# Moving the probability scaling of the first attention from VectorE to GpSimd

## The chip, the cores and the metric

One core of a Trainium2 chip runs the whole program as one launch. The metric is the device time of that launch in microseconds. Between kernels, medians of several runs are compared. One further execution of the kernel was recorded by the profiler, and all rows and durations below come from it.

The engines are called by the names the profile uses: PE is TensorE, PEld its weight loads, DVE is VectorE, ACT is ScalarE, POOL is GpSimd, SP is SyncE.

## What is computed

The reference is a chain of two models over 256 tokens of width 1024. The first has an RG-LRU mixer, a convolutional feed-forward part, a sparse attention mixer (`nsa_mixer`) and another feed-forward part. The second has two layers with a convolution branch, neighbourhood attention and grouped attention, and a gated feed-forward part. The change touches `nsa_mixer` only. Cut to what matters:

```python
q, kv = heads of (x @ w_in)              # 16 query heads of width 64, 4 key/value heads
gates = sigmoid(...)                     # three gates for each head and token
# branch 0: compressed keys (done before the loop that the change touches)
# branch 1: chosen key blocks; with 256 tokens every block is chosen
s = q @ k_sel.T - slope * dist
p = masked_softmax(s, dist >= 0)
o_sel = p @ v_sel
# branch 2: a window of 512 keys; with 256 tokens it holds all earlier keys
s = q @ k_win.T - slope * dist
p = masked_softmax(s, m_w)
o_win = p @ v_win
o = gates[0] * o_cmp + gates[1] * o_sel + gates[2] * o_win
```

For branches 1 and 2 the kernel multiplies each row of exponentials by one number, the reciprocal of the row's sum times the gate of that branch, head and token, so that the two products with the values can be added up in one PSUM bank.

## The kernel before, in words

Each engine has its own instruction stream, written out in its own function, and the streams meet at semaphores. Weights stream from HBM through a ring of four slots, which SP fills. Most stages are three-pass products of split weights: ACT rounds a job of weights (`w_hi`), DVE subtracts (`w_lo`, L1353), and PE multiplies (all by the helper at L579). In the feed-forward stages POOL splits the hidden activations into two parts (a cast at L520, a subtraction at L522). While `ffn_out0` and `nsa_out` run it also sums squares of the residual (L530, L534), and it issues a few small loads.

The attention loop of `nsa_mixer` is called `softmax` in each engine's stream. It walks over 16 **pairs**. A pair is two heads for one tile of 128 queries. Even pairs have query tile 0 and see 128 keys, odd pairs have query tile 1 and see 256 keys, and each head has two branches, so a pair holds four blocks of 128x128 or of 128x256. Two pairs make a **round** in this text. In step v of their loops the engines do:

- **PE:** the scores of pair v (into two PSUM banks; the two bank pairs of `score_pairs` alternate); on even v from 4 on, the products with the values of pairs v-4 and v-3 (one output bank); then the transposes of pair v-2 (L781), which wait on `prob_ready` and write `turn_pair`, of which there is only one.
- **DVE:** for pair v, two instructions that add slope times distance to the scores in PSUM (L1524) and one that takes the row maxima (L1535, signals `score_max`); then for pair v-1 the reciprocal of the four sums (L1545), its product with the gates (L1550), and four multiplications of a block by its factor (L1555), which signal `prob_ready` for each head.
- **ACT** (all by the helper at L1020): the copy of the transposed pair v-2 from PSUM (signals `turned_ready`), then four exponentials of pair v into `s_p`, each with its row sum (signals `prob_exp`); on odd v from 5 on, the copy of a finished output bank.
- **POOL:** nothing. It waits for the last output copy (`o_free`, L546) and then issues two loads (L548) for later work.

`s_p` has four places, two for each pair. So the exponentials of pair v overwrite those of pair v-2. ACT is safe to do so since its own copy of the transposed pair v-2 comes first in its stream:

```python
go(used_pair(pT[...]), used_pair(turn_pair, kind, q), ACT.Copy).then_inc(turned_ready, 1)
if v < pairs:
    act.wait_ge(score_max, base // 2 + v + 1)
```

`s_sum` and `s_rec` hold the sums and factors of two pairs.

The functions that the change touches, with the profile's line numbers:

Of the kernel before, what the change touches and what calls it, by code (L numbers as in the profile page):

```python
# [27 lines left out]
ALU = mybir.AluOpType  # L28
# [260 lines left out]
def program(nc, wstream, params_in, consts_in, rpb_in, c_in, x_in, out):  # L289
    ctx = ExitStack()  # L290
    with ctx:
# [3 lines left out]
        def sem(name):  # L295
            return ctx.enter_context(nc.semaphore(name))
# [120 lines left out]
        operand_ready = sem("operand_ready")  # L417
        act_operand_ready = sem("act_operand_ready")
        score_full, score_max, prob_exp, prob_ready = (sem(n) for n in ("score_full", "score_max", "prob_exp", "prob_ready"))
        turned_full, turned_ready, o_full, o_free = (sem(n) for n in ("turned_full", "turned_ready", "o_full", "o_free"))  # L420
        dve_step, act_step, pool_step = sem("dve_step"), sem("act_step"), sem("pool_step")
        c_landed, c_ready, mod_summed = sem("c_landed"), sem("c_ready"), sem("mod_summed")
# [85 lines left out]
        @block.gpsimd  # L508
        def _(pool):
            for e in range(2):  # L510
                nc.gpsimd.memset(mod_parts[:, :, e, :], 0.0).then_inc(pool_written, 1)
            pstep = Count()

            def split_hidden(stage, units, products, hidden, N):

                for n, j, i in steps(pool, units, (pstep, 2)):
                    for e in range(2):
                        hi, lo = (v[:, bass.ds(n * 2 + e, 1), :].rearrange("p a b -> p (a b)")[:, 0:N] for v in hidden)
                        pool.wait_ge(acc_free[2 + e], n + (USED[stage][2 + e] + 1))
                        nc.gpsimd.tensor_copy(hi, products[:, e, 0:N]).then_inc(pool_step, 1)  # L520
                        pool.wait_ge(pool_step, pstep.next())
                        nc.gpsimd.tensor_tensor(lo, products[:, e, 0:N], hi.bitcast(F32), ALU.subtract).then_inc(pool_written, 1)  # L522


            def sum_squares(stage):

                for m in range(KD):
                    b, n = out_bank(stage, m)
                    pool.wait_ge(acc_free[b], n + (USED[stage][b] + 1))
                    square = nc.gpsimd.tensor_tensor((sq_one if m else sq_sum), x[:, m, 0:S], x[:, m, 0:S], ALU.mult)  # L530
                    if m:
                        square.then_inc(pool_step, 1)
                        pool.wait_ge(pool_step, pstep.next())
                        square = nc.gpsimd.tensor_tensor(sq_sum, sq_sum, sq_one, ALU.add)  # L534
                    if m < KD - 1:
                        square.then_inc(pool_step, 1)
                        pool.wait_ge(pool_step, pstep.next())
                    else:
                        square.then_inc(squares_summed, 1)

            pool.wait_ge(operand_ready, KL)
            for s in range(2):
                pool.dma_start(n_c[s], c_in[s]).then_inc(c_landed, 16)
            split_hidden("ffn_in0", KF1 // 2, f_prod, f_hidden, S)
            sum_squares("ffn_out0")
            pool.wait_ge(o_free, len(attention_jobs()) // 4)  # L546
            for s in range(2):
                pool.dma_start(n_c[s], c_in[s]).then_inc(c_landed, 16)  # L548
            sum_squares("nsa_out")
            split_hidden("ffn_in1", KF1 // 2, f_prod, f_hidden, S)  # L550

            for l in range(DEPTH):
                pool.wait_ge(rpb_place, l + 1)
                pool.dma_start(a_rpb.rearrange("p a b -> p (a b)"), rpb_in[l]).then_inc(rpb_landed, 16)
                pool.wait_ge(rpb_landed, 16 * (l + 1))
                pool.wait_ge(consts_landed, 16)

                nc.gpsimd.tensor_tensor(a_rpb, a_rpb, con("na_mask", 0, GRID).unsqueeze(1).broadcast_to([P, 48, GRID]),
                                        ALU.add).then_inc(rpb_ready, 1)
                if l == 0:  # L560

                    pool.wait_ge(o_free, (len(attention_jobs()) + len(attention_jobs(0))) // 4)
                    for s in range(2):
                        pool.dma_start(a_c[s], c_in[s]).then_inc(c_landed, 16)
                    pool.wait_ge(acc_free[3], USED["branch01"][3] + 2)
                    pool.dma_start(m_c[0], c_in[0]).then_inc(c_landed, 16)
                for p, units in (("a", HALF_A), ("b", HALF_B)):
                    split_hidden(f"mlp_in{l}{p}", units, m_prod, m_hidden, S2 if l == 0 else S)
# [735 lines left out]
        def _(dve):  # L1304
# [3 lines left out]
            def link(ins):  # L1308

                ins.then_inc(dve_step, 1)  # L1310
                dve.wait_ge(dve_step, step.next())
# [195 lines left out]
            def softmax(layer=None):  # L1507

                jobs = attention_jobs(layer)
                pairs = len(jobs) // 2  # L1510
                base = jobs_done.base
                for v in range(pairs + 1):
                    if v < pairs:
                        kind, t, _, q = jobs[2 * v]
                        if kind == "na" and jobs[2 * v - 1][0] != "na":
                            dve.wait_ge(rpb_ready, layer + 1)
                        dve.wait_ge(score_full, base // 2 + v + 1)
                        if kind == "nsa":
                            nk = (q + 1) * P
                            c = con("causal", q * S, nk).unsqueeze(1).broadcast_to([P, 2, nk])  # L1520
                            for p in range(2):
                                slope = float(np.float32(2.0 ** (-8.0 * (head_of(kind, t, p) + 1) / HEADS)))
                                sc = used(score_pairs[v % 2][:, p, :], kind, q)
                                ins = V.scalar_tensor_tensor(out=sc, in0=c, scalar=slope, in1=sc, op0=ALU.mult, op1=ALU.add)  # L1524
                            link(ins)
                        if kind == "na" and q < 2:
                            for p in range(2):
                                head = 2 * t + p
                                bias = a_rpb[:, head * 6 + 2 - 2 * q:head * 6 + 6 - 2 * q, :].rearrange("p a b -> p (a b)")
                                sc = score_pairs[v % 2][:, p, 0:S]  # L1530
                                ins = V.tensor_tensor(sc, sc, bias, ALU.add)
                            link(ins)
                        i = (v % 2) * 4
                        top = s_max[:, i:i + 4] if kind == "nsa" else s_max[:, i:i + 4:2]
                        ins = V.tensor_reduce(top, used_pair(score_pairs[v % 2], kind, q), AX, ALU.max, negate=True)  # L1535
                        if kind == "gqa":
                            link(ins)
                            ins = V.tensor_tensor(top, top, head_root[:, 8 * q + 2 * t:8 * q + 2 * t + 2], ALU.mult)
                        ins.then_inc(score_max, 1)
                    if v >= 1:  # L1540
                        kind, t, _, q = jobs[2 * v - 2]
                        i = ((v - 1) % 2) * 4
                        dve.wait_ge(prob_exp, base + 2 * v)
                        r_ = s_rec[:, i:i + 4] if kind == "nsa" else s_rec[:, i:i + 4:2]
                        link(V.reciprocal(r_, s_sum[:, i:i + 4] if kind == "nsa" else s_sum[:, i:i + 4:2]))  # L1545
                        if kind == "nsa":

                            g = n_gate[:, q, HEADS:3 * HEADS].rearrange("p (b h) -> p h b", b=2)[:, head_of(kind, t, 0):head_of(kind, t, 1) + 1:GROUP, :]
                            r2 = r_.rearrange("p (h b) -> p h b", b=2)
                            link(V.tensor_tensor(r2, r2, g, ALU.mult))  # L1550
                        for p in range(2):
                            o = used(s_p[:, (2 * v - 2 + p) % 4, :], kind, q)
                            for br in range(2 if kind == "nsa" else 1):
                                c = i + 2 * p + br
                                ins = V.tensor_scalar(o[:, br, :], o[:, br, :], s_rec[:, c:c + 1], None, ALU.mult)  # L1555
                            ins.then_inc(prob_ready, 1)
                jobs_done.base += len(jobs)

            ffn(0)
# [413 lines left out]
```

## Time and profile before

| | |
|---|---|
| median of 3 runs | 2247.96 us (2245.68 to 2248.45) |
| the profiled execution | 2248.55 us, of which 2246.7 us is the span of the trace |
| PE busy | 2103.2 us (94% of the span) |
| DVE busy | 1514.9 us (67%) |
| ACT busy | 875.6 us (39%) |
| POOL busy | 249.5 us (11%), 231 instructions |
| first attention | about 449.5 to 511 us of the span |

The span is the time from the first to the last recorded instruction. The busy shares are averages over the whole program and say little about a stage of some 60 us. For that, the trace is asked for the chain of waits and for the instructions in that stretch.

### The profile page before, as it was taken

The numbers are of one execution on the slowest core, as the hardware profiler recorded it, in microseconds if no ns is written. First come the engines' busy times: TensorE is split into PE (matmuls) and PEld (weight loads), VectorE is DVE, ScalarE is ACT, GpSimd is POOL, SyncE is SP. The second block draws the span as 40 slices with busy tenths as digits, with TensorE's granted clock in tenths as the row PEclk, the third lists the DMA queues.
The fourth block names the chain that finished last, engine by engine and source line by source line (L and its number), as shares of the span: only waits on it lengthen the run. The fifth ranks groups of instructions, "written<-read, shape, count | busy, mean of one in ns | idle before, by whom it ended". The sixth has DMA issues, their size and how long they took to land.

```text
span 2246.7 us, 33659 instructions
## 1 busy us (share of the span) xinstructions
PE 2103.2 (94%) x12858; PEld 1791.8 (80%) x12858; DVE 1514.9 (67%) x2859; ACT 875.6 (39%) x1376; POOL 249.5 (11%) x231
## 2 busy tenths in 40 slices
PE   7899999879999799889899989999997998999998
PEld 6789999748999588646567568888886865998998
DVE  7658898395888669776698863383276966355554
ACT  4634444273444432475211242212214336435443
POOL 0003321003330010000000002201211000001220
PEclk9999999889999899999999999999998999999999
DMA  6345465404556322103455422252243310344552
GB/s 234 121 175 190 179 248 209 149 1 165 188 179 260 134 95 76 57 1 132 152 213 207 170 111 94 93 193 107 94 169 123 131 57 20 151 176 162 186 187 78
DMA packets 46987, 318.09 MB, mean 142 GB/s; under 512 B 5008, under 2 KB 8080, under 8 KB 9488
## 3 DMA queue, kind: packets, MB, share of 16 engines
q1 hardware_dynamic: 45568, 309.58, 37.4%
q0 software_dynamic: 1296, 6.82, 0.8%
q8 instruction: 84, 1.38, 0.2%
q14 instruction: 39, 0.32, 0.0%
HBM read 315.33 MB, written 1.05 MB: 141 GB/s over the span
## 4 chain that ended last, share of the span: by engine, by line
PE 72%; DVE 17%; ACT 5%; issue 3%; DMA 2%; DVEq 0%; ACTq 0%; SPq 0%
PE ps L579 68%; DVE ps L1373 4%; DVE w_lo L1353 4%; ACT arena L1020 3%; DMA ring<-wstream 2%; PE ps L781 2%; PE ps L627 1%; DVE arena L1337 1%; DVE small L1535 1%; DVE rs L1319 1%; DVE arena L1555 1%; DVE h_lo L1347 1%; ACT w_hi L1020 1%; ACT L1020 1%; DVE ps L1524 1%
## 5 line engine op out<-in xcount | busy, mean ns | idle before, releaser
L579 PE MATMUL ps<-h_hi,w_hi 128*128 128x256 f32 (+1 forms) x2616 | 849.2, 325 | 48.7 <-DVE h_lo L1347 30.7
L579 PE MATMUL ps<-h_lo,w_hi 128*128 128x256 f32 (+1 forms) x2616 | 834.9, 319 | 0.0
L579 PE MATMUL ps<-h_hi,w_lo 128*128 128x256 f32 (+1 forms) x2616 | 833.8, 319 | 0.0
L1353 DVE TENSOR_TENSOR w_lo<-ring,w_hi 128x1024 fp32r<-128x1024 f32 x433 | 545.2, 1267 | 356.5 <-ACT w_hi L1020 355.7
L1020 ACT ACTIVATE w_hi<-ring 128x1024 fp32r<-128x1024 f32 x433 | 452.3, 1055 | 582.0 <-PE ps L579 476.6
L579 PEld LDWEIGHTS ps<-h_hi,w_hi 128*128 128x128 f32 x2616 | 503.0, 192 | 98.7 <-issue 42.9
L579 PEld LDWEIGHTS ps<-h_lo,w_hi 128*128 128x128 f32 x2616 | 504.6, 193 | 33.2 <-issue 1.2
L579 PEld LDWEIGHTS ps<-h_hi,w_lo 128*128 128x128 f32 x2616 | 504.5, 193 | 33.0
L1020 ACT ACTIVATE arena<-ps 128x512 f32<-128x512 f32 (+2 forms) x246 | 140.9, 575 | 461.1 <-PE ps L579 415.1
L1373 DVE SCALAR_TENSOR_TENSOR ps<-ring,arena 128x512 f32<-128x512 f32 x384 | 250.8, 725 | 0.0
L579 PE MATMUL ps<-arena,ring 128*128 128x256 f32 (+2 forms) x840 | 217.6, 420 | 20.6 <-DMA ring<-wstream 7.8
L579 PE MATMUL ps<-hid_hi,w_hi 128*128 128x256 f32 (+1 forms) x736 | 224.6, 305 | 0.9 <-DVE w_lo L1353 0.9
L579 PE MATMUL ps<-hid_lo,w_hi 128*128 128x256 f32 (+1 forms) x736 | 224.3, 305 | 0.0
L579 PE MATMUL ps<-hid_hi,w_lo 128*128 128x256 f32 (+1 forms) x736 | 224.3, 305 | 0.0
L579 PEld LDWEIGHTS ps<-arena,ring 128*128 128x128 f32 x840 | 150.9, 193 | 84.2 <-issue 54.5
L520 POOL CAST hid_hi<-arena 128x256 f32 (+3 forms) x92 | 82.5, 897 | 1024.8 <-DVE arena L1471 1024.8
L579 PE MATMUL ps<-arena 128*64 128x256 f32 (+4 forms) x800 | 129.5, 449 | 28.4 <-ACT arena L1020 24.7
L579 PEld LDWEIGHTS ps<-hid_hi,w_hi 128*128 128x128 f32 x736 | 138.4, 188 | 9.4 <-issue 1.2
L579 PEld LDWEIGHTS ps<-hid_lo,w_hi 128*128 128x128 f32 x736 | 138.1, 188 | 8.2
L579 PEld LDWEIGHTS ps<-hid_hi,w_lo 128*128 128x128 f32 x736 | 138.0, 188 | 8.1
L1687 DVE SCALAR_TENSOR_TENSOR arena<-arena,prm 128x512 f32<-128x512 f32 (+1 forms) x240 | 129.9, 613 | 0.4
L579 PEld LDWEIGHTS ps<-arena 128*64 128x64 f32 (+1 forms) x800 | 63.4, 174 | 70.4 <-issue 37.4
(153 smaller groups left out, 1673.3 us busy)
## 6 DMA issues: line engine op xcount, KB each, us to landing
ring<-wstream SPq DMA_DIRECT2D x290, 1024.0 KB, 4.8
arena<-c_in POOLq DMA_DIRECT2D x7, 512.0 KB, 4.5
arena<-rpb POOLq DMA_DIRECT2D x2, 1536.0 KB, 8.2
x<-x_in SPq DMA_DIRECT2D x2, 1024.0 KB, 12.1
out<-arena SPq DMA_DIRECT2D x8, 128.0 KB, 2.0
cst<-consts SPq DMA_DIRECT2D x1, 928.0 KB, 11.9
prm<-params SPq DMA_DIRECT2D x1, 580.0 KB, 10.6
ring<-wstream SPq DMA_DIRECT2D x1, 512.0 KB, 3.5
```

The lines of the kernel that those rows point to most:

```text
L520: nc.gpsimd.tensor_copy(hi, products[:, e, 0:N]).then_inc(pool_step, 1)
L579: ins = nc.tensor.matmul(*a, **k)
L627: ins = nc.tensor.matmul(psO[:, 0:N], ones[:], sq[:, k % 4, 0:N], start=k == 0, stop=k == KD - 1)
L781: ins = nc.tensor.transpose(turn_pair[:, p, b * P:(b + 1) * P], s_p[:, (2 * u + p) % 4, b * P:(b + 1) * P], ident)
L1020: return nc.scalar.activation(o, i, f, **k)
L1319: link(V.reciprocal(rs[:, 0:N], rs[:, 0:N]))
L1337: V.scalar_tensor_tensor(out=scaled[:, n % 8, :], in0=x[:, k, c], scalar=gain(k, s), in1=rs[:, c], op0=ALU.mult, op1=ALU.mult).then_inc(sc ...
L1347: ins = V.scalar_tensor_tensor(out=h_lo[:, k, c], in0=t, scalar=bias(k, s), in1=hi, op0=ALU.add, op1=ALU.subtract)
L1353: V.tensor_tensor(w_lo[:, job % SPLITS, :], raw_job(job), w_hi[:, job % SPLITS, :].bitcast(F32), ALU.subtract).then_inc(weights_ready, 1)
L1373: V.scalar_tensor_tensor(out=ps[4 + p][:], in0=w, scalar=1.0, in1=c[s][:, p * S2:(p + 1) * S2], op0=ALU.mult, op1=ALU.mult, accum_out=mod_ ...
L1524: ins = V.scalar_tensor_tensor(out=sc, in0=c, scalar=slope, in1=sc, op0=ALU.mult, op1=ALU.add)
L1687: return V.scalar_tensor_tensor(out=cy[:, c, 0:ns, :], in0=a_u3[:, c, 0:ns, bass.ds(j, S)], scalar=w, in1=cy[:, c, 0:ns, :], op0=ALU.mult, ...
```

## The change

POOL gets a loop over the 16 pairs. For each pair it waits for `factor_ready`, multiplies the four blocks of `s_p` by their factors in place, and signals `prob_ready` for each head. DVE no longer multiplies the blocks in this attention. It signals `factor_ready` at the gate product, without waiting for its own result, and from the third pair of factors on it waits until POOL has used the factors that it is about to overwrite. In the later attentions (kinds `gqa` and `na`) DVE multiplies as before.

```diff
+        factor_ready = sem("factor_ready")
...
             sum_squares("ffn_out0")
+            nsa_jobs = attention_jobs()
+            for v in range(len(nsa_jobs) // 2):
+                kind, _, _, q = nsa_jobs[2 * v]
+                pool.wait_ge(factor_ready, v + 1)
+                for p in range(2):
+                    o = used(s_p[:, (2 * v + p) % 4, :], kind, q)
+                    for br in range(2):
+                        c = (v % 2) * 4 + 2 * p + br
+                        ins = nc.gpsimd.tensor_scalar(o[:, br, :], o[:, br, :], s_rec[:, c:c + 1], None, ALU.mult)
+                    ins.then_inc(prob_ready, 1)
             pool.wait_ge(o_free, len(attention_jobs()) // 4)
...
                         dve.wait_ge(prob_exp, base + 2 * v)
+                        if kind == "nsa" and v >= 3:
+                            dve.wait_ge(prob_ready, 2 * v - 4)
...
-                            link(V.tensor_tensor(r2, r2, g, ALU.mult))
+                            V.tensor_tensor(r2, r2, g, ALU.mult).then_inc(factor_ready, 1)
+                        if kind == "nsa":
+                            continue
                         for p in range(2):
-                            o = used(s_p[:, (2 * v - 2 + p) % 4, :], kind, q)
-                            for br in range(2 if kind == "nsa" else 1):
-                                c = i + 2 * p + br
-                                ins = V.tensor_scalar(o[:, br, :], o[:, br, :], s_rec[:, c:c + 1], None, ALU.mult)
-                            ins.then_inc(prob_ready, 1)
+                            o, c = used(s_p[:, (2 * v - 2 + p) % 4, :], kind, q), i + 2 * p
+                            V.tensor_scalar(o[:, 0, :], o[:, 0, :], s_rec[:, c:c + 1], None, ALU.mult).then_inc(prob_ready, 1)
```

## Rows read from the trace of the kernel before

**Rows 1.** The page's chain that ended last, shares of the whole span.

```profile
PE 72%; DVE 17%; ACT 5%; issue 3%; DMA 2%; DVEq 0%; ACTq 0%; SPq 0%
```

**Rows 2.** Who waited for whom, 450 to 502 us: total us, times, longest.

```profile
PEld ps L781 <- DVE arena L1555: 11.7, 8, 1.9
```

**Rows 3.** The chain from 488 us on: start us, us, what ran.

```profile
488.50 0.88 DVE arena L1555 x4
489.37 0.68 DVE ps L1524 x2
...
490.08 0.69 DVE small L1535
...
490.89 0.17 DVE small L1550
...
491.09 1.14 DVE arena L1555 x4
...
495.00 0.88 DVE arena L1555 x4
...
501.22 1.94 ACT arena L1020 x8
...
503.60 1.15 DVE arena L1555 x4
...
504.80 1.11 PE ps L781 x8
...
507.09 3.52 PE ps L579 x20
...
510.63 0.39 ACT arena L1020
```

**Rows 4.** Timeline, ACT: start us, us, engine, line, operation, tiles, forms, [idle before <-releaser].

```profile
461.39 1.02 ACT L1020 ACTIVATE arena<-ps 128x1024 f32<-128x1024 f32 x1 [1.91 <-PE ps L781]
462.31 0.47 ACT L1020 ACTIVATE arena<-ps,small 128x256 f32<-128x256 f32 x1
```

**Rows 5.** Operations on the tile hid_hi, 540 to 780 us: ns min/median/max.

```profile
L520 POOL CAST hid_hi<-arena x24: 398/1274/1447, 554.7 to 681.3; 128x256 f32 x24
L522 POOL TENSOR_TENSOR hid_lo<-arena,hid_hi x24: 732/739/747, 556.1 to 681.9; 128x256 f32 x24
```

**Rows 6.** POOL's groups by form: xcount | busy us, mean ns | idle before.

```profile
L520 POOL CAST hid_hi<-arena 128x512 f32 x20 | 12.2, 612 | 369.1 <-DVE arena L1471 369.1
```

**Rows 7.** Timeline at 514 to 516 us, DVE and POOL.

```profile
514.83 0.42 DVE L1409 TENSOR_TENSOR x<-x,ps 128x256 f32<-128x256 f32 x1 [10.09 <-PE ps L579]
...
515.34 0.61 POOL L530 TENSOR_TENSOR arena<-x 128x256 f32<-128x256 f32 x1 [2.90 <-DVE x L1409]
```

**Rows 8.** Timeline in the second feed-forward part, DVE and POOL.

```profile
556.10 0.74 POOL L522 TENSOR_TENSOR hid_lo<-arena,hid_hi 128x256 f32 x1 [0.17 <-POOL hid_hi L520]
...
610.56 1.22 DVE L1353 TENSOR_TENSOR w_lo<-ring,w_hi 128x1024 fp32r<-128x1024 f32 x1
...
610.83 1.20 POOL L520 CAST hid_hi<-arena 128x256 f32 x1 [7.02 <-DVE arena L1471]
```

**Rows 9.** Timeline of PE through one round.

```profile
488.07 1.95 PE L579 MATMUL ps<-arena 128*64 128x256 f32 x20 [0.57 <-ACT arena L1020]
489.96 0.66 PE L781 MATMUL ps<-cst,arena 128*128 128x128 f32 x4
490.54 1.13 PE L579 MATMUL ps<-arena 64*128 64x512 f32 x4
492.28 1.09 PE L781 MATMUL ps<-cst,arena 128*128 128x128 f32 x8 [0.61 <-DVE arena L1555]
...
494.58 0.87 PE L579 MATMUL ps<-arena 128*64 128x256 f32 x6 [0.57 <-ACT arena L1020]
```

**Rows 10.** Windows of a round here and of a later attention: length, busy us of each engine, granted PE clock.

```profile
482.87:489.37 6.50, 5.32 (x42) 3.36 (x40) 6.29 (x19) 5.22 (x20) 0.00 (x0) 1.00 0.00 0
1014.00:1028.00 14.00, 9.90 (x68) 5.97 (x68) 7.43 (x20) 9.59 (x25) 0.00 (x0) 1.00 0.00 0
```

## The prediction

> **What bounds the kernel now.** I read the page's chain first, to see where DVE matters at all: PE carries 72% of it and DVE 17% [rows 1]. The chain cut to 488 us and later shows part of that 17%. Until 501.2 us it holds nothing but DVE: multiplications, bias, maxima, reciprocal, gates, and again [rows 3]. A round (one even and one odd pair) lasts from 488.50 to 495.00, so 6.50 us, of which the blocks' multiplications are 0.88 + 1.14 = 2.02 us. The waits say the same: in 52 us PE's transposes waited 11.7 us for DVE's multiplications [rows 2]. In one round of 6.50 us DVE is busy 6.29, PE 5.32, ACT 5.22 and POOL 0 [rows 10].
>
> So the tempting sum is 8 rounds by 2.02 us, 16 us less. It fails if something else stands close behind DVE. The chain after 501.22, where DVE has no scores left, shows what: exponentials, reciprocal, gates, multiplications, transposes, copy, one after the other [rows 3]. In the loop that string closes to a ring, because `s_p` has places for two pairs only. The exponentials of pair v come behind ACT's copy of pair v-2.
>
> **The ring, before.** For odd pairs, which are the larger: 2.38 from the first exponential at 501.22 to the multiplications at 503.60 (exponentials 1.94, the rest reciprocal and gates), 1.20 from there to the transposes at 504.80, transposes 1.11 [rows 3], and from the copy's start to the next exponential 0.92 [rows 4]. The sum is 5.61 us a round. It hides below DVE's 6.50 with 0.89 to spare.
>
> **The change, part by part.**
>
> *DVE* loses 2.02 us a round and its self-wait at the gate product, and stands at about 4.5. It is no bound any more.
>
> *The ring* loses the 1.20, and the self-wait of 0.03 between gate product and multiplications (490.89 and 0.17 to 491.09) [rows 3]. It gets: signal and wake-up of POOL 0.09 (515.34 less 514.83 and 0.42) [rows 7]; four POOL multiplications, 4t; and POOL's signal to PE. No row shows that signal. DVE's to PE takes 0.05 (504.80 less 503.60 and 1.15) [rows 3], and POOL's to itself 0.17 [rows 8]. I take 0.10 between them. The ring becomes 5.61 - 1.20 - 0.03 + 0.09 + 0.10 + 4t = **4.57 + 4t**. It equals the old round at t = 0.48 us.
>
> *The price t of a 128x256 multiplication on POOL* has no row. Nearest from below is the cast, also with one tensor in and one out: 0.40 where nothing disturbed it [rows 5]. From above, POOL's own multiply of two tensor inputs takes 0.61 [rows 7], and its subtraction 0.74 [rows 5]. The new instruction reads one tensor like the cast, but has a factor to fetch and an arithmetic step like the square. I can't place it nearer to either and take the middle, t = 0.505. For 128 columns: the cast takes 0.61 at 512 columns [rows 6] and 0.40 at 256, so 0.84 ns a column on 0.18, and 0.29 at 128. The square on the same 0.18 gives 0.40. The middle is 0.35.
>
> *The floor* without any POOL cost is a second loop, on PE. The value products start at 488.07 and take 1.89 to the even transposes at 489.96, then 0.58 to the odd scores, those 1.13, and from odd transposes to the next value products 2.30 (492.28 to 494.58) [rows 9]. That is 5.90 a round. The round can't become shorter than this whatever POOL costs.
>
> *The even ring* has exponentials, transposes and copy of half the width and is below the odd one. It costs nothing while the odd one binds.
>
> *Filling.* In the first steps PE paces the loop. There the first pair's multiplications lie open: 0.09 + 4 x 0.35 + 0.10 against 0.03 + 0.88 + 0.05, so +0.63.
>
> *Rounds.* From the exponentials of pair 3 at 462.31 [rows 4] to those of pair 15 at 501.22 [rows 3] there are six rounds in 38.91 us, 6.49 each. After: 4.57 + 4 x 0.505 = 6.59, so 6 x 0.10 = +0.6.
>
> *Emptying.* Behind the last exponentials the string lies open once: 0.09 + 0.10 + 2.02 = 2.21 against 1.23, so +0.98.
>
> *Waits and queues.* DVE's new wait on `prob_ready` stands ahead of a reciprocal, with the next pair's bias and maxima queued behind it. It asks for factors used two pairs ago, whose transposes have long run, so nothing. On POOL the two loads (L548) come behind the new loop, but they waited for the last output copy at 510.63 anyway. SP's queue is not touched and no transfer runs in this stretch (DMA share 0.00) [rows 10]. The stage after the attention starts on PE when the last output copy has ended, so a delay goes through to the end in full.
>
> **Sum:** 0.63 + 0.6 + 0.98 = **+2.2 us** on the execution's 2248.55. In t, with the 128-wide price moving along, it is nearly 28t - 12. The median of runs is 0.6 below that execution. I add to the median: 2250.2.
>
> **A page against the rows.** The four casts and squares above put POOL at 0.84 to 1.7 ns a column. The Trainium skill, GPSIMD Engine Reference, section "Elementwise — side-by-side cycle accounting", gives 1.8 cycles per element as the best case of a tight loop, at 1.2 GHz. By an estimate from that page the instruction would take 0.57 and 0.37 us with the 0.18 of the casts, and the sum would be +4.1, to 2252.1. The cast's rows disagree for one input (1.0 cycle by the same clock), and no run here shows a multiplication by a factor.
>
> **Rivals.**
>
> *POOL's ring becomes clearly longer than DVE's round.* It decides from t = 0.59. At the square's 0.61 the ring is 7.01: fill 4 x 0.40 + 0.19 - 0.96 = +0.8, rounds 6 x 0.52 = +3.1, end +1.4, together +5.3, to 2253.3. At the subtraction's 0.74 it is +9.3, to 2257.3, and a multiplication of 1 us would give some +17. For it: the arithmetic rows. Against: those read two tensors.
>
> *POOL and DVE get in each other's way.* Next to DVE's `w_lo` subtraction of two SBUF tensors a cast that takes 0.40 alone took 1.20 and ended with it [rows 8]. In the new loop DVE's gate product also has two SBUF inputs (factors and gates). If it met POOL's multiplications for the pair before, one would wait for an instruction of the other, up to t in every pair: about 6 x 0.5 + 0.5 = +3.5 on top, to 2253.7. Against it: gate products are 2.6 us apart (490.89, and 0.20 ahead of the multiplications at 488.50) [rows 3], and an even pair needs POOL for 1.4. The other DVE work reads PSUM and at most one SBUF tensor. The Trainium skill, SBUF — State Buffer, section "Who interferes with whom", has this as a lock for two-input instructions against a reading GpSimd. By this rule the trace agrees for the cast.
>
> *POOL costs little more than DVE did, t = 0.33 or less.* Then PE's loop binds: 6 x (5.90 - 6.49) = -3.5, with fill and end about +0.4, so -3.1, to 2244.9. For it: POOL idles here, with nothing to disturb it. Against: no row of POOL at 256 columns is below 0.40. At 0.40 itself the sum is -0.9. To be faster by more than 0.2% a part of the floor would have to be wrong.
>
> *PE's clock drops* if PE idles more. With a round of 6.6 PE is busy for 5.3, 80%. A later attention has PE busy 9.90 of 14.00 us at granted clock 1.00 [rows 10], so I give it little. The value products at the end, after a pause, took 3.52 us [rows 3] against 1.95 [rows 9]; such a PE would make the loop of 5.90 about 10 and cost some +21.
>
> **How the numbers follow.** About 0.2%, 4.5 us, is what a measurement of this kernel can tell from no change. Forecast (t between 0.40 and 0.58): 0.52. Cheaper, down to the floor: 0.05. POOL's price above 0.58: 0.33. The two-input conflict: 0.05. Clock: 0.02. Floor wrong and faster: 0.03. Same is 0.57, slower 0.40, faster 0.03. The range goes from 2245 (near the floor) to 2261 (t about 0.9), which leaves out some 0.12.
>
> **What would show it.** Right: DVE at about 4.5 busy in a round, with idle time ahead of the reciprocal; POOL's multiplications near 0.35 and 0.5; PE's transposes waiting for POOL; the chain going round exponentials, factors, POOL, transposes, copy; odd exponentials 6.6 us apart. Wrong: DVE still in the chain, PE waiting for copies alone (floor), POOL instructions stretched next to the gate products, or a granted clock below 1 in the steady part.

## The result, and the profile after

The changed kernel takes 2269.59 us (median of 4 runs, 2267.03 to 2271.24) against 2248.2 us for the kernel before in the same comparison. The ratio is 1.0094, with a 95% interval of 1.0077 to 1.0112. That is 21 us slower, where +2.2 was forecast and 2261 was the upper end of the range. In a second comparison, with 15 runs of the kernel before beside it, the ratio was 1.0081 (1.0067 to 1.0095): 18 us. The profiled execution of the first comparison has a span of 2265.2 us, 18.5 more than before. Both ratios lie far outside what the runs scatter by.

The price of the new instruction first. Groups of POOL by form, 440 to 530 us of the changed kernel (x count | busy us, mean ns | idle before it, and who ended the idle time):

```profile
L555 POOL TENSOR_SCALAR arena<-arena,small 128x256 f32<-128x256 f32 x32 | 29.0, 924 | 6.7 <-DVE small L1563 6.7
L555 POOL TENSOR_SCALAR arena<-arena,small 128x128 f32<-128x128 f32 x32 | 18.8, 604 | 109.3 <-DVE small L1563 109.3
```

A multiplication of 128x256 takes 0.92 us, of 128x128 0.60. Four in a row take 3.63 us, 0.91 each, since each starts a little before the last one has ended. Forecast were 0.505 and 0.35. The value does not lie between the cast's 0.40 and the subtraction's 0.74 [rows 5], but above both.

Now the chain of the changed kernel, one round and the start of the next (start us, us, what ran; three gaps of 0.02 are left out):

```profile
482.13 2.86 ACT arena L1031 x9
...
485.01 0.19 DVE small L1558
...
485.22 0.18 DVE small L1563
485.40 0.08 issue
485.48 3.63 POOL arena L555 x4
489.12 0.04 issue
489.16 1.11 PE ps L792 x8
...
490.29 2.86 ACT arena L1031 x9
```

This is the ring of the prediction, piece for piece: copy and exponentials, reciprocal, gate product, four POOL multiplications, transposes, copy again. It takes 490.29 - 482.13 = 8.16 us, where the chain of before went through DVE alone and took 6.50 [rows 3]. Without POOL's 3.63 it is 4.53; the forecast was 4.57. In the six rounds of the forecast DVE is busy for 4.3 to 4.8 us each, where about 4.5 was forecast.

Who waited for whom in the changed kernel, 450 to 525 us (total us, times, longest):

```profile
PEld ps L792 <- POOL arena L555: 24.6, 11, 3.5
...
DVE ps L1535 <- PE ps L590: 21.3, 13, 3.4
```

The transposes, which waited 11.7 us for DVE's multiplications before [rows 2], now wait 24.6 us for POOL's. DVE waited 1.9 us for scores before (450 to 512 us); now it is 21.3. It has been relieved and has nothing to do with the time it got.

Where the 18.5 us of the two spans lie: the attention, from the first scores on PE to the end of the last output copy, takes 61.5 us before (449.55 to 511.02) and 76.9 after (452.41 to 529.30). That is 15.4. The other 3.1 lie outside it: 2.9 ahead of the first scores, where the instructions are the same in both kernels, and 0.2 behind the last copy (1735.7 and 1735.9 us to the end of the span).

### The profile page after: what moved, and what is told of

Same layout as the page of the kernel before. It is cut to its first block, busy times and chain, and to the rows that moved or that the text cites. A ratio compares the mean times of both kernels' runs of the same rounds, so it can differ in the third digit from the quotient of the medians.

```text
span 2265.2 us, 33675 instructions
## 1 busy us (share of the span) xinstructions
PE 2111.5 (93%) x12858; PEld 1796.7 (79%) x12858; DVE 1499.5 (66%) x2795; ACT 875.6 (39%) x1376; POOL 297.0 (13%) x295
## 4 chain that ended last, share of the span: by engine, by line
PE 72%; DVE 16%; ACT 5%; issue 3%; DMA 2%; POOL 1%; DVEq 0%; ACTq 0%; SPq 0%
PE ps L590 68%; DVE ps L1384 4%; DVE w_lo L1364 4%; ACT arena L1031 4%; PE ps L792 2%; DMA ring<-wstream 2%; PE ps L638 1%; POOL arena L555 1%; DVE arena L1348 1%; DVE rs L1330 1%; DVE h_lo L1358 1%; ACT w_hi L1031 1%; ACT L1031 1%; DVE arena L1699 1%; DVE arena L1504 1%
## 5 line engine op out<-in xcount | busy, mean ns | idle before, releaser
L1031 ACT ACTIVATE w_hi<-ring 128x1024 fp32r<-128x1024 f32 x433 | 452.4, 1055 | 584.7 <-PE ps L590 478.3
L590 PE MATMUL ps<-arena 128*64 128x256 f32 (+4 forms) x800 | 135.9, 468 | 27.8 <-ACT arena L1031 23.8
```

The source lines that it names most:

```text
L590: ins = nc.tensor.matmul(*a, **k)
L1031: return nc.scalar.activation(o, i, f, **k)
```

## The experiments

The theory under test (A): the time of a round is that of a ring of some 4.5 us plus four POOL instructions, so the size of t explains the loss. Each profile gives the attention as above, and the round from the starts of the exponentials of odd pairs. Each kernel is compared with runs of the kernel before that were made beside it. Their median is 2250.83 us for the first four experiments, 2250.87 for the one with POOL on the even pairs and the three with three places, and 2250.63 for the others. The edits are shortened.

**POOL copies instead of multiplying.**

```diff
-ins = nc.gpsimd.tensor_scalar(o[:, br, :], o[:, br, :], s_rec[:, c:c + 1], None, ALU.mult)
+ins = nc.gpsimd.tensor_copy(o[:, br, :], o[:, br, :])
```

> The changed kernel, but GpSimd copies each block in place instead of multiplying it (it leaves out the scaling by reciprocal and gate). Theory A, a ring of 4.57 us plus four POOL instructions sets the round of two pairs: the cast form took 0.40 us for 128x256, so the ring is 6.2 us, the round 6.2 to 6.4 against 8.16 in the changed kernel, and the time returns to that of the kernel before, 2247 to 2250. Rival B, the work being on POOL at all is what costs (signals, a lock between the engines): the round stays near 8 and the time above 2262. Rival C, the lower clock of PE carries a third or more of the loss: the time stops near 2254.

Measured: 2250.96 us against 2250.83 before, ratio 1.000 (0.9991 to 1.001). Attention 60.0 us, round 6.19 on average over six. The signals and the work on POOL are all there and the loss is gone, so B has fallen; and the time does not stop near 2254, so C does not carry a third of the loss.

**A constant factor.**

```diff
-... s_rec[:, c:c + 1], None, ALU.mult)
+... 0.5, None, ALU.mult)
```

> The changed kernel with the constant 0.5 in place of the factor that is read from SBUF (it leaves out the scaling by reciprocal and gate). If fetching the factor is what makes the POOL instruction 0.90 us instead of the 0.40 of a cast, it falls to about 0.45 us, and the time to 2248 to 2251. If the multiply form itself is slow, it stays at 0.85 to 0.90 us for 256 columns, the round at 8.0 to 8.2 and the time at 2267 to 2271.

Measured: 2262.33 us, ratio 1.0051 (1.0034 to 1.0068). Attention 71.2, round 7.81. The time lies between the two answers that were written down.

**The tensor-tensor form.**

```diff
-ins = nc.gpsimd.tensor_scalar(o[:, br, :], o[:, br, :], s_rec[:, c:c + 1], None, ALU.mult)
+ins = nc.gpsimd.tensor_tensor(o[:, br, :], o[:, br, :], s_rec[:, c:c + 1].broadcast_to([P, (q + 1) * P]), ALU.mult)
```

> The changed kernel with the same product written as a tensor-tensor multiplication whose second input is the factor, repeated along the columns. Theory A with the price of the square seen before (0.61 us for 256 columns, about 0.40 for 128): ring 4.57 + 2.44 = 7.0 us, time about 2253.5, some 16 us better than the changed kernel. If POOL needs as long for it as for the scalar form (0.9 us), 2269.

Measured: 2256.55 us, ratio 1.0027 (1.0017 to 1.0038). Attention 65.7, round 6.85. It computes the same as the changed kernel in 12 us less (5.7 above the kernel before, where the changed kernel is 18.1 above it in the larger comparison).

The POOL groups of the three, in this order (x count | busy us, mean ns | idle before):

```profile
L555 POOL COPY arena<-arena 128x256 f32<-128x256 f32 x32 | 11.4, 401 | 8.8 <-DVE small L1563 8.8
L555 POOL COPY arena<-arena 128x128 f32<-128x128 f32 x32 | 8.0, 293 | 119.6 <-DVE small L1563 119.6
```

```profile
L555 POOL TENSOR_SCALAR arena<-arena 128x256 f32<-128x256 f32 x32 | 26.3, 848 | 7.2 <-DVE small L1563 7.1
L555 POOL TENSOR_SCALAR arena<-arena 128x128 f32<-128x128 f32 x32 | 16.1, 527 | 110.9 <-DVE small L1563 110.9
```

```profile
L555 POOL TENSOR_TENSOR arena<-arena,small 128x256 f32<-128x256 f32 x32 | 18.6, 615 | 7.5 <-DVE small L1563 7.5
L555 POOL TENSOR_TENSOR arena<-arena,small 128x128 f32<-128x128 f32 x32 | 11.8, 402 | 113.7 <-DVE small L1563 113.7
```

Each pair of rows gives a slope and a constant. Copy: 0.84 ns a column on 0.19 us. Two tensors: 1.66 on 0.19. Constant factor: 2.51 on 0.21. Factor from SBUF: 2.50 on 0.28. So fetching the factor costs 0.08 us an instruction, once; the rest of the high price is the scalar form's time per column, three times that of the copy.

And the four instructions in the chain of each, first with the constant factor, then with two tensors:

```profile
476.98 3.30 POOL arena L555 x4
...
484.79 3.30 POOL arena L555 x4
```

```profile
482.42 2.34 POOL arena L555 x4
...
489.27 2.34 POOL arena L555 x4
```

The rounds are 7.81 = 3.30 + 4.51, 6.85 = 2.34 (rounded) + 4.51, and 8.16 = 3.63 + 4.53. The formula holds over three prices with one constant. With the copy (four in 1.44 us) it would give 5.95. Three of the six rounds there took 5.93 or 5.94 and the other three 6.39 to 6.48, so another limit takes turns with it.

**POOL takes only the odd pairs, DVE the even ones** (with a semaphore of its own for each engine).

```diff
+                if not on_pool(v):        # on_pool(v) is v % 2 == 1
+                    continue
```

> GpSimd multiplies only the odd pairs (256 keys), VectorE the even ones. Theory A, the ring of the odd pairs binds and the even pairs on POOL cost only their exposed place at the start and a little queueing: 40% of POOL's work goes, the round stays at 8.16 us, the attention shortens from 76.9 to about 75 us, and the time is 2267 to 2268. Rival D, POOL's total work (5.96 us in a round) sets the pace: the round falls by about the 2.34 us taken away and the time to 2256 or less.

Measured: 2267.13 us, ratio 1.0073 (1.0057 to 1.009), within 2 us of the changed kernel's time, as expected. The timeline of ACT, the first exponential of two odd pairs in a row:

```profile
482.57 0.47 ACT L1044 ACTIVATE arena<-ps,small 128x256 f32<-128x256 f32 x1
...
490.74 0.47 ACT L1044 ACTIVATE arena<-ps,small 128x256 f32<-128x256 f32 x1
```

8.17 us. POOL does 3.6 us of work in a round instead of 5.96 and at most 2 us come back. D has fallen: the odd pairs' latency sets the pace, not POOL's load. (The attention took 78.2 us here rather than 75; four of its six rounds took 8.16 to 8.17 and the other two 8.66 and 8.44. Their granted clocks were 0.88 and 0.90, but a round of 8.17 had 0.89. What sets the two apart is where the stretch of lower clock fell: their odd transposes, which are part of the ring, took 1.59 and 1.37 us instead of 1.09, and that is all of the 0.50 and 0.28 that they are longer. From the first scores to the exponentials of pair 3 it took 15.1 us, against 14.1 and 14.9 in the two profiles of the changed kernel.)

**POOL takes only the even pairs, DVE the odd ones** (the same edit with `v % 2 == 0`).

> GpSimd multiplies only the even pairs (128 keys), VectorE the odd ones. Theory A: the odd ring is that of the kernel before (5.61 us), the even ring with four POOL instructions of 0.585 us is 5.5, VectorE is busy about 5.6 in a round, PE's loop takes 5.90. The round is 5.9 to 6.0 us against 6.49 before: -3.5 over six rounds, +1.6 for the first pair's exposed multiplications, together about -2, so 2245 to 2248. Rival B (any work on POOL costs) gives 2253 or more.

Measured: 2256.5 us, ratio 1.0025 (1.0014 to 1.0037), attention 65.4, round 7.09. I expected 5.9 and a gain. The time alone would fit B; the copy on POOL had ruled that out, and the chain of this kernel names what I had missed:

```profile
485.59 2.35 POOL arena L563 x4
487.94 0.04 issue
487.98 0.66 PE ps L805 x4
488.64 1.08 PE ps L598 x4
...
489.75 1.31 DVE ps L1548 x2
...
491.07 0.04 DVE small L1559
491.11 1.11 issue
492.21 0.18 DVE small L1571
...
492.42 0.18 DVE small L1576
...
492.67 2.35 POOL arena L563 x4
```

There is a second ring, made of instruction order. The even transposes wait for POOL. The next odd scores stand behind them in PE's stream. DVE's bias and maxima wait for those scores, and the next even pair's reciprocal stands behind them in DVE's stream. (The row of 1.11 us marked "issue" is the rest of the odd pair's maxima, which run from 491.07 for 1.22 us.) It takes 4.73 us plus POOL's four 128-wide multiplications, 7.08 in all.

**The same, with the even transposes behind the odd scores in PE's stream.**

```diff
-                    if 2 <= v < pairs + 2:
-                        u = v - 2
+                    for u in [v - 3, v - 2] if v % 2 else []:
```

> GpSimd on the even pairs only, as in the run where the round came out at 7.09 us instead of 5.9; but PE issues the even pair's transposes behind the next odd pair's scores instead of ahead of them. Theory F: in that run a second ring bound the round, which goes through PE's order: POOL's even multiplications 2.35, even transposes 0.66, odd scores 1.08, bias 1.30, maxima 1.15, reciprocal, gates, POOL again, 7.09 in all. With the transposes out of the scores' way it is cut: round 5.9 to 6.3, the attention 59 to 61.5 us instead of 65.4, the time within 2 us of the kernel before. If the loss there has another cause, the round stays near 7.

Measured: 2253.8 us, ratio 1.0014 (1.0005 to 1.0023), attention 63.2, round 6.69. The second ring is cut and POOL has left the chain, but only 0.4 us of a round came back and not 0.8 to 1.2, the attention missed the expected 59 to 61.5, and the time is 3.2 us above the kernel before and not within 2. The chain of this kernel now repeats ACT's exponentials, PE's scores and value products, transposes, exponentials.

```profile
485.05 2.42 ACT arena L1046 x9
...
487.61 3.01 PE ps L598 x24
490.62 0.60 PE ps L807 x4
```

So F holds for what bound that run, since POOL's multiplications are gone from the chain and the round is shorter; my number for what would bind next was too low.

**Three places of pairs instead of two, POOL on all pairs.** The third place lies in memory that is free by then; transposes, copies and value products come one pair later.

```diff
+        more_p = part(2048, 2, S2)
...
-                    if 2 <= v < pairs + 2:
-                        u = v - 2
+                    if lag <= v < pairs + lag:      # lag = 3
+                        u = v - lag
...
-s_p[:, (2 * u + p) % 4, ...]
+place(kind, 2 * u + p)[:, ...]                      # one of 6
```

> The changed kernel with three places of pairs for the probabilities instead of two, and transposes, copies and value products one pair later, so that the exponentials of a pair no longer wait for the pair two before but three before. POOL's instructions are as before. Theory A: the ring of 8.2 us now spans three pairs, that is about 5.5 us a round, and no longer binds; POOL itself does, with 5.96 us of work in a round, about 6.2 with its wake-ups. Six rounds of 2 us come back, so 12 of the 21 us: 2256 to 2259. If the ring is not what costs, the time stays at 2268 to 2272.

Measured: 2249.85 us against 2250.87, ratio 0.9997 (0.9988 to 1.0007). The attention is 63.2 us, the round 6.11. POOL's instructions cost as much as in the changed kernel (0.93 and 0.61 us), and by the medians all of the loss is gone, where 12 us of it were expected back. The round came out as expected. By the one profile the attention is 13.7 us shorter than in the changed kernel and still 1.7 to 3.2 longer than before; the rest of what the medians gained is not explained. The window 470 to 482 us of this kernel (length, busy us of PE, PEld, DVE, ACT, POOL, granted clock):

```profile
470.00:482.00 12.00, 10.39 (x82) 6.18 (x80) 8.95 (x20) 9.80 (x39) 11.90 (x17) 1.00 0.00 1
```

POOL is busy 11.90 of 12.00 us, so its throughput would allow no shorter round. But the chain of this kernel does not pass through POOL. It repeats PE's scores and value products (3.01 us), the even transposes, ACT's copy and exponentials, and PE again. Two limits have met here at 6.11 us.

**Three places, POOL on the even pairs only.**

> Both together: three places of pairs, GpSimd the even pairs only and VectorE the odd ones. Neither ring binds, POOL has 2.34 us in a round, VectorE 5.6, PE 5.3, ScalarE 5.2. Theory A: round 5.6 to 5.9 us against 6.49 before, 2243 to 2247, possibly the best of all. Rival: PE's loop over value products, transposes, scores and copy holds it at 5.9, then 2246.

Measured: 2251.51 us, ratio 1.0006 (0.9996 to 1.0015), attention 60.1, round 6.14. POOL is down to 4.70 of 12 us and the round is no shorter than with all pairs on POOL. Both numbers expected (5.6 to 5.9 or 5.9, and 2243 to 2247) were too low. The chain is the same loop of PE and ACT, and this run shows that it alone holds the round at 6.14:

```profile
485.45 3.01 PE ps L604 x24
488.46 0.60 PE ps L812 x4
...
489.08 0.56 ACT arena L1051
...
489.98 1.57 ACT arena L1051 x7
...
491.59 3.01 PE ps L604 x24
```

**Control: three places, DVE multiplies everything.**

> Control: the kernel before (VectorE multiplies everything) with three places of pairs. VectorE had 6.29 of 6.50 us busy in a round, so a longer ring gives nothing: 2247 to 2250, round 6.50. If the ring already cost something before, it is faster by 3 us or more.

Measured: 2253.3 us, ratio 1.0008 (0.9994 to 1.0022), round 6.50 as expected, attention 63.9. The deeper ring alone gives nothing. The time is 2.4 us above the kernel before and 3 above the range expected, and the attention 2.4 to 3.9 longer: the loop has an extra step at its ends, which the expectation left out. But the interval still includes no change.

**PE kept busy in the rounds.**

```diff
+                                if q == 1 and v >= 4:
+                                    mm(... the scores of this head, once more into the same bank)
                                 ins = mm(...
```

> The changed kernel with the scores of each odd pair from the fifth on computed twice into the same place, so that PE idles some 0.9 us less in a round, at a point of the round where nothing waits for it (odd transposes wait 2.26 us for POOL there). Theory A: PE's clock matters little inside the rounds; those that took 8.49 us become 8.16, so at best 1 us is gained, and the time stays within 1.5 us of the changed kernel. Rival C, the clock carries the part of the loss that the ring does not: the granted clock is 1.00 through the attention and 4 to 7 us come back.

Measured: 2267.28 us against 2268.73 for the changed kernel beside it; attention 76.6 us. The same window in the changed kernel, where it holds most of a slow round, and here (length, busy us of PE, PEld, DVE, ACT, POOL, granted clock):

```profile
494.00:506.00 12.00, 8.10 (x46) 4.45 (x47) 6.25 (x13) 7.11 (x28) 9.23 (x12) 0.86 0.00 1
```

```profile
494.00:506.00 12.00, 8.62 (x57) 4.84 (x56) 6.25 (x13) 7.11 (x28) 9.39 (x12) 1.00 0.01 2
```

The granted clock stays at 1.00 from 470 to 518 us and the rounds from 475 us on are all 8.16. The median is 1.4 us lower, with ranges that overlap (2264.7 to 2269.7, and 2266.3 to 2271.9 for the changed kernel), and the attention 0.3 and 0.7 us shorter than in the two profiles of the changed kernel. With the clock held up inside the rounds, 16.7 us of the loss are still there. C has fallen as a main cause.

**Both kernels profiled a second time.**

> The changed kernel once more, beside many runs of the kernel before on one chip. Its first profile puts 15.4 us of the loss inside the attention (76.9 against 61.5 us) and 3.1 us outside, at places that the change does not touch. Theory A: those 3.1 us are chance of one execution, so the medians differ by 15 to 18 us and the attention again takes 76 to 78 us. Rival E, something outside the attention is lost every time: 20 us or more, and again over 1788 us of span outside the attention.

> The kernel before once more, for a second profile. Theory A: attention 61.5 us, rounds of 6.50; outside the attention 1785 to 1790 us of span, as the kernels with and without work on POOL have shown. Rival E: 1785 again, below all kernels that use POOL.

Measured: the changed kernel 2268.73 us, 18.1 more than the 2250.63 beside it; attention 77.4 us. The kernel before: attention 60.0. The difference of the attentions is 17.4 us, that of the first profiles 15.4. Outside the attention the spans are 2185.2 and 2189.7 us (before), 2188.3 and 2192.2 (after), and 2184.6 to 2189.7 in the ten variants. (The two expectations say 1785 to 1790; they are 400 us too low by a slip in a subtraction.)

Where the difference outside lies can be told more closely. From the end of the last output copy to the end of the span it is 1735.7 and 1736.7 us before, 1735.9 and 1736.1 after. So nothing is lost behind the attention. What differs is the time up to the first scores: 449.6 and 453.1 us before, 452.4 and 456.1 after, 449.9 to 453.0 in the variants. No work was moved there, and the two values of one kernel lie 3.5 and 3.7 us apart, more than the kernels do. Of the signs of E, the loss of 20 us did not come (18.1), but the span outside was again above that of the kernel before (2192.2). I take the 3 us for chance; the 456.1 alone lies above all others, and it stays unexplained.

## Why the prediction was wrong

**The step that failed** is "the price t of a 128x256 multiplication on POOL". I put t at 0.505 between the cast and the square; the four take 3.63 us, 0.91 each. With that one number exchanged, and 0.59 for 128 columns, the same working gives: filling 0.09 + 2.35 + 0.10 - 0.96 = +1.6, rounds 6 x (4.57 + 3.63 - 6.49) = +10.3, emptying 0.19 + 3.63 - 1.23 = +2.6, together +14.4. Measured in the attention, first and second pair of profiles: filling +1.3 and +2.1, rounds +10.6 and +10.2, emptying +3.5 and +5.1, together +15.4 and +17.4. The bracketing was wrong in kind: I ordered the instructions by how many tensors they read, and the scalar form, with one input, is slower than both two-input forms.

**What held.** DVE bound the loop and is relieved of 2 us a round. The ring is the one of the prediction, in its parts and its constant (4.57 forecast, 4.53 measured). POOL's signals took 0.08 to start and 0.04 to PE, against 0.09 and 0.10. The two runs on either side of the break-even of 0.48 fit the working: the copy at 0.40 ends at no change, where -0.9 had been worked out, and the two-input form at 0.61 at +5.7 us, where it was +5.3. The fill does lie exposed: from the first scores to the exponentials of pair 3 it is 12.76 us before and 14.09 after, +1.33, or +2.1 in the second profiles.

**The Trainium skill against the rows.** The estimate from 1.8 cycles a column (the Trainium skill, GPSIMD Engine Reference, section "Elementwise — side-by-side cycle accounting") was 0.57 us for 256 columns. Measured were 0.92 us, with a slope of 2.5 ns a column, 3.0 cycles at the 1.2 GHz given there. For this instruction the measurement decides.

**Rivals.** The first one, POOL's ring becoming clearly longer than DVE's round, is what happened, with a price outside the rows that it was worked out from; the line "a multiplication of 1 us would give some +17" was the nearest. I ended the range at 2261, t of about 0.9. With the measured t the working gives 2262.4, just outside; the measured 2269.6 lies 7 us further on, of which what follows accounts for a part. The conflict between the engines did not come: no POOL multiplication took more than 0.93 us, and gate products keep their duration, but for one of 16 (DVE, operations on the factor tiles: ns min/median/max):

```profile
L1563 DVE TENSOR_TENSOR small<-small,arena x16: 165/166/316, 458.1 to 518.2; 128x4 f32<-128x4 f32 x16
```

Where POOL has the even pairs only, the odd pair's gate product ran beside one of its multiplications and took 0.28 us instead of 0.17, which is far from a wait of a whole multiplication. The argument for this rival misread its row in part: the cast [rows 8] ended at 612.03, 0.25 us behind the subtraction's end at 611.78, and not with it.

The clock came in part. Once the loop had filled, one transposing step of an odd pair took 1.43 us instead of 1.09, and the last one 1.98; the granted clock was 0.55 from 516 to 530 us. The rival's price of +21 has the size of the measured loss by coincidence only: in the run with the clock at 1.00 nearly all of the loss stayed. The slower last steps belong to the 1 to 3 us that the exchanged number leaves open. The chance of one execution belongs to it too, since the last value products of the kernel before took 3.50 us in its first profile and 1.95 in its second:

```profile
507.09 3.50 PE L579 MATMUL ps<-arena 128*64 128x256 f32 x20 [1.21 <-ACT arena L1020]
```

```profile
510.67 1.95 PE L579 MATMUL ps<-arena 128*64 128x256 f32 x20 [1.20 <-ACT arena L1020]
```

**A step that was wrong and cost nothing here.** I wrote that the even ring costs nothing while the odd one binds. True for its own parts, but the even multiplications sit in the second ring of 4.73 us plus their time. At 7.08 it stays below the 8.16 of the changed kernel. It set the round where POOL took only the even pairs.

The floor of 5.90 was also a little low. With the ring opened, PE and ACT together held the round at 6.11 and 6.14, and none of the ten variants was measurably faster than the kernel before, the one with POOL's instructions at 0.40 us included.

## What to carry to other kernels

When a busy engine is relieved of a step, look for the ring that the step is part of: how many buffers close it, and what its latency becomes on the new engine. Here 2 us of DVE time a round were paid for with 2.5 us more in a ring that had 0.9 to spare, and one more buffer undid the loss with the instruction as slow as it was. A faster form of the same product gave back 12 of 18 us. Neither made the kernel faster than it had been: the faster form left the ring at 6.85 us, above DVE's old 6.50, and with the ring opened the next limit stood at 6.11, so that six rounds gained 2.3 us and the longer end of the loop took them back. An instruction with no row of its own is not bracketed by rows that look alike. Here a single run of it would have given the price, and the ordering by inputs gave a wrong one.

## What was not expected of the hardware

On POOL a multiplication of a 128x256 tile by one number for each partition took 0.92 us, and the same product with that number repeated as a second tensor 0.615; with a constant it took 0.85, a copy 0.40. Among these four the scalar form is the slowest, at 2.5 ns a column against 1.66 and 0.84.
